# State outputs of an S5 layer in groups of 16 channels, turned back through DRAM

## The chip, the cores and the metric

The kernel runs on one core of a Trainium2 chip. The metric is the device time of one execution in microseconds. TensorE multiplies matrices (weights loaded into the array, columns streamed past them, sums in PSUM, eight banks of 512 float32 columns on 128 partitions). VectorE, ScalarE and GpSimd do the elementwise work; SyncE (SP) and ScalarE issue DMAs.

## The reference, cut to what matters

Two layers on 528 tokens (16 meta tokens and 512) of width 1024. Each layer is: half an FFN, a projection `x @ w_in` that feeds three mixers (attention with latent q and kv, a short gated convolution, an S5 state space branch), a gated merge, and half an FFN. All in float32.

```python
def s5_branch(u, a_re, a_im, log_dt, b_re, b_im, c_re, c_im, d, w_glu, b_glu, w_out):
    ...   # ab = exp(dt * a), bb = coef * b, both complex
    bu_re = jnp.einsum('gnh,blgh->blgn', bb_re, uf)
    bu_im = jnp.einsum('gnh,blgh->blgn', bb_im, uf)
    _, _, xr, xi = lax.associative_scan(_ssm_combine, elems, axis=1)
    y = (jnp.einsum('ghn,blgn->blgh', c_re, xr) - jnp.einsum('ghn,blgn->blgh', c_im, xi) + d * uf)
    y = jax.nn.gelu(y.reshape(B, L, S5_WIDTH))
    y = y * jax.nn.sigmoid(y @ w_glu + b_glu)
    return y @ w_out
```

There are 32 groups of 16 channels with 64 complex states each.

## The kernel before, in words

Features lie on partitions, tokens along the free dimension, in two halves of 264. Every large product takes its weights in chunks of 128 output features: SP loads a chunk into one of two raw buffers (L481), ScalarE rounds it (`round_ahead`, L1318), GpSimd makes the rest (`split`, L611), and TensorE makes three products (rounded by rounded, rounded by rest, rest by rounded; `product`, L696). The rounded weights sit in four slots, so ScalarE works three chunks ahead. Semaphores order everything; each engine has a program of its own, written out in the order in which it runs.

The S5 branch cuts the 528 tokens into 66 chunks of 8 steps. State inputs of a chunk are made from an input that eight small DMAs have stacked on partitions (`u8`, L1605; `s5_states_in`, L986). VectorE scans over the 66 chunks (L2245) and turns the states back, four pairs of groups at a time (`scan_turned_back`, L2248). The output of a chunk has two parts: a Toeplitz part from the eight steps of the same chunk, and a part from the state at its start. The Toeplitz kernels are made by `s5_toeplitz` (L1016), on all 128 channels of a tile at once with zeros between the groups, just before the tenth of twelve convolution chunks, and ScalarE copies them (`take_toeplitz`, L1561) into `K`, which VectorE has cleared (L2456). `s5_outputs` on TensorE (L1030) makes, for each of four tiles of 128 channels, the Toeplitz products (L1044, 128-column weights) and the state products (L1051, 32-column weights), both with the step along the free dimension. VectorE adds the skip term `d * u` (L2309), ScalarE applies Gelu in place, VectorE splits the result into rounded and rest (L2316, L2317), and TensorE goes on with `values` (V of the attention, L1076) and `glu` (L719).

The parts of the chain that the change and the prediction's steps touch:

- TensorE, in `conv` (L998): twelve chunks; `CONV_PAIR` gives each a pair of PSUM banks, and a chunk waits (`conv_taken`) until VectorE has taken the chunk that used the pair before. Chunk 12 uses the pair of chunk 10.
- VectorE, L2444 to L2467: for each tile of the convolution `conv_first` (copies the first chunk of the tile) and `conv_tile`; between them `scan_turned_back`, `latents_begin` (two reciprocals, L2293 and L2295) and, behind the last tile, `latent_tiles` (L2297).
- The tables: `tables_beside` (L2054) places the steps of the input tables (`in_step`), of the turning factors (`turn_step`) and of the output tables (`out_step`, L2176) beside the first FFN's tiles. The first FFN has three parts with 6, 8 and 8 tiles; the tables' transposes (`turn_inputs`, L950) stand behind the down products of part 2.
- SP's order of loads (L558 to L595), GpSimd's order of splits (L649 to L663), ScalarE's order (L1590 to L1652).

## Time and profile before

| | us |
|---|---|
| median of 3 runs | 2581.45 (2578.11 to 2581.68) |
| span of the profiled execution, whose own time is this span | 2579.4 |
| TensorE busy | 2543.4 |
| VectorE busy | 1414.7 |
| ScalarE busy | 953.8 |
| GpSimd busy | 1223.7 |
| first layer, end of the ninth convolution chunk to first GLU product | 54.1 |

The profile is one execution. Its timeline gives the start and length of the instructions of an engine, merged where neighbours are of the same kind; a bracket holds the idle time before them and what ended it. A float32 product appears as two instructions.

### The profile page before, as it was taken

The numbers are of one execution on the slowest core, as the hardware profiler recorded it, in microseconds if no ns is written. First come the engines' busy times: TensorE is split into PE (matmuls) and PEld (weight loads), VectorE is DVE, ScalarE is ACT, GpSimd is POOL, SyncE is SP. The second block draws the span as 40 slices with busy tenths as digits, with TensorE's granted clock in tenths as the row PEclk, the third lists the DMA queues.
The fourth block names the chain that finished last, engine by engine and source line by source line (L and its number), as shares of the span: only waits on it lengthen the run. The fifth ranks groups of instructions, "written<-read, shape, count | busy, mean of one in ns | idle before, by whom it ended". The sixth has DMA issues, their size and how long they took to land.

```text
span 2579.4 us, 51328 instructions
## 1 busy us (share of the span) xinstructions
PE 2543.4 (99%) x20356; PEld 2420.4 (94%) x20356; DVE 1414.7 (55%) x2475; ACT 953.8 (37%) x1694; POOL 1223.7 (47%) x708
## 2 busy tenths in 40 slices
PE   9999999999999999999999999999999999999997
PEld 9999999998899999999999999999977788989897
DVE  6665433874453484535576654339744535835356
ACT  4222224235532242636352222242355322437363
POOL 4444434413234456868554444354132345568582
PEclk9999999999999999999999999999999999999998
DMA  5333333312233333333233323333122333334332
GB/s 165 92 92 88 90 90 91 91 28 66 53 84 89 95 91 98 95 102 100 82 110 97 92 82 92 88 91 94 26 66 54 83 98 98 92 86 127 82 99 82
DMA packets 457391, 227.16 MB, mean 88 GB/s; under 512 B 42385, under 2 KB 456337, under 8 KB 457201
## 3 DMA queue, kind: packets, MB, share of 16 engines
q1 hardware_dynamic: 450880, 217.09, 30.9%
q10 hardware_dynamic: 6320, 7.41, 1.1%
q8 instruction: 135, 2.21, 0.4%
q14 instruction: 56, 0.45, 0.1%
HBM read 220.20 MB, written 2.10 MB: 86 GB/s over the span
## 4 chain that ended last, share of the span: by engine, by line
PE 92%; DVE 3%; issue 2%; POOL 1%; ACT 1%; DMA 0%; ACTq 0%; POOLq 0%; DVEq 0%; SPq 0%
PE ps L696 64%; PE ps L830 14%; PE ps L806 4%; PE ps L719 3%; PE ps L1044 1%; PE ps L1129 1%; PE ps L1168 1%; POOL w_lo L611 1%; PE ps L1133 1%; PE ps L1051 1%; PE ps L1144 1%; DVE ln_in L1856 0%; ACT ln_in L1300 0%; DMA w_raw<-in_ffn_w_gate 0%; PE ps L1146 0%
## 5 line engine op out<-in xcount | busy, mean ns | idle before, releaser
L611 POOL TENSOR_TENSOR w_lo<-w_raw,w_hi 128x1024 fp32r<-128x1024 f32 (+4 forms) x400 | 851.3, 2135 | 1135.9 <-ACT w_hi L1300 1135.5
L1300 ACT ACTIVATE w_hi<-w_raw 128x1024 fp32r<-128x1024 f32 (+4 forms) x400 | 372.7, 936 | 640.5 <-PE ps L696 401.6
L696 PE MATMUL ps<-x_hi,w_hi 128*128 128x264 f32 (+2 forms) x2720 | 396.5, 296 | 0.3 <-ACT w_hi L1300 0.3
L696 PE MATMUL ps<-x_hi,w_lo 128*128 128x264 f32 (+2 forms) x2720 | 389.3, 293 | 0.8 <-POOL w_lo L611 0.8
L696 PE MATMUL ps<-x_lo,w_hi 128*128 128x264 f32 (+2 forms) x2720 | 389.0, 293 | 0.0
L696 PEld LDWEIGHTS ps<-x_hi,w_hi 128*128 128x128 f32 x2720 | 355.1, 188 | 14.5 <-issue 0.8
L696 PEld LDWEIGHTS ps<-x_hi,w_lo 128*128 128x128 f32 x2720 | 355.3, 188 | 11.5 <-POOL w_lo L611 1.7
L696 PEld LDWEIGHTS ps<-x_lo,w_hi 128*128 128x128 f32 x2720 | 355.4, 188 | 9.8
L1896 DVE TENSOR_TENSOR ps<-hid_rest,ps 128x528 f32<-128x528 f32 (+1 forms) x56 | 39.7, 710 | 238.4 <-PE ps L696 226.8
L696 PE MATMUL ps<-hid_hi,w_hi 128*128 128x264 f32 (+1 forms) x1008 | 158.2, 301 | 0.1
L696 PE MATMUL ps<-hid_hi,w_lo 128*128 128x264 f32 (+1 forms) x1008 | 156.6, 299 | 0.0
L696 PE MATMUL ps<-hid_lo,w_hi 128*128 128x264 f32 (+1 forms) x1008 | 156.4, 299 | 0.0
L611 POOL TENSOR_TENSOR w_lo<-w_sum,w_hi 128x512 fp32r<-128x512 f32 x90 | 118.7, 1324 | 78.0 <-ACT w_hi L1300 77.5
L611 POOL TENSOR_TENSOR w_lo<-w_pair,w_hi 128x512 fp32r<-128x512 f32 x108 | 145.1, 1359 | 9.7 <-ACT w_hi L1300 9.7
L696 PEld LDWEIGHTS ps<-hid_hi,w_hi 128*128 128x128 f32 x1008 | 137.1, 188 | 6.7 <-DVE ln_in L1917 0.5
L696 PEld LDWEIGHTS ps<-hid_hi,w_lo 128*128 128x128 f32 x1008 | 137.2, 188 | 6.3
L696 PEld LDWEIGHTS ps<-hid_lo,w_hi 128*128 128x128 f32 x1008 | 136.9, 188 | 6.2
L1300 ACT ACTIVATE hid_rest<-ps 128x528 f32 (+2 forms) x88 | 51.0, 603 | 176.4 <-PE ps L696 163.8
L2415 DVE SCALAR_TENSOR_TENSOR stat<-stat,ps 128x528 f32<-128x528 f32 (+1 forms) x32 | 22.2, 695 | 158.1 <-PE ps L696 158.1
L1300 ACT ACTIVATE w_hi<-w_sum 128x512 fp32r<-128x512 f32 x90 | 56.4, 631 | 101.1 <-DVE w_sum L1960 66.7
L830 PE MATMUL ps<-turned_lo,w_hi 128*128 128x264 f32 (+1 forms) x576 | 92.6, 283 | 0.0
L830 PE MATMUL ps<-turned_hi,w_hi 128*128 128x264 f32 (+1 forms) x576 | 92.5, 282 | 0.0
(352 smaller groups left out, 4397.8 us busy)
## 6 DMA issues: line engine op xcount, KB each, us to landing
w_raw<-in_w_in SPq DMA_DIRECT2D x82, 512.0 KB, 3.9
w_raw<-in_ffn_w_down SPq DMA_DIRECT2D x64, 512.0 KB, 3.7
w_raw<-in_ffn_w_up SPq DMA_DIRECT2D x56, 512.0 KB, 3.8
w_raw<-in_ffn_w_gate SPq DMA_DIRECT2D x48, 512.0 KB, 3.8
w_pair<-in_ffn_w_gate SPq DMA_DIRECT2D x40, 512.0 KB, 5.2
w_pair<-in_ffn_w_up SPq DMA_DIRECT2D x32, 512.0 KB, 5.2
w_raw<-in_ffn_w_down SPq DMA_DIRECT2D x32, 384.0 KB, 3.3
w_raw<-in_w_o SPq DMA_DIRECT2D x16, 512.0 KB, 3.7
```

The lines of the kernel that those rows point to most:

```text
L611: pool.tensor_tensor(held(w_lo, c), src, held(w_hi, c).bitcast(f32), ALU.subtract).then_inc(w_split, 1)
L696: ins = nc.tensor.matmul(dst, wk, x[:, k0 + k, tokens], start=first and k == 0 and n == 0, stop=last and k == n_tiles - 1 and n == 2)
L719: ins = nc.tensor.matmul(dst, held(w, c + j, k * P, (k + 1) * P), x[:, k, tokens], start=k == 0 and n == 0, stop=k == nk - 1 and n == 2)
L806: ins = nc.tensor.matmul(ps[:, bank, 0:sp.half], held(w, c + d, k * P, (k + 1) * P), x[:, k, sp.halves[h]], start=p == 0 and k == 0, stop= ...
L830: ins = nc.tensor.matmul(ps[:, banks + bank, 0:sp.half], held(w, c + n, k * P, (k + 1) * P), x[:, k], start=start and i == 0 and k == 0, s ...
L1044: nc.tensor.matmul(ps[:, a + bank, (s0 - lo) * NC:4 * NC], K[:, m, j, :], ug[:, s0 - j:up - j, m, :], start=j == 0, stop=False, skip_group ...
L1051: ins = nc.tensor.matmul(ps[32 * q:32 * q + 32, a + s // 4, (s % 4) * NC:(s % 4 + 1) * NC], cl[:, s, ri, p * 32:(p + 1) * 32], X[:, ri, p, :],
L1129: ins = nc.tensor.matmul(ps[0:nq, j % 2, 0:q0 + nq], qT[:, b, q0:q0 + nq], kT[:, b, 0:q0 + nq], start=True, stop=True)
L1133: ins = nc.tensor.matmul(ps[0:nq, h, 0:HALF], qT[:, b, q0:q0 + nq], kT[:, b, h * HALF:(h + 1) * HALF], start=True, stop=True)
L1144: nc.tensor.transpose(ps[:, 2 + buf, k * P:(k + 1) * P], pr[:, buf, k * P:(k + 1) * P], ident[:])
L1300: return nc.scalar.activation(out, in_, f, **kw)
L1896: st.done(tt(up, gate, up, MUL))
```

## The change

The Toeplitz kernels are made earlier, for groups of 16 channels alone: on TensorE ahead of part 3 of the first FFN (`s5_kernels`), each from 64 rows of states. ScalarE copies them to `Kc` (`take_kernels`), and 16 DMAs on SP's queue, placed between the loads of convolution chunks, lay them out as the block Toeplitz matrices `T` that GpSimd has cleared. The skip term is added into the kernels by eight products with the identity. In `s5_outputs` the eight steps of a group lie stacked on the partitions, so that the Toeplitz part takes 32-column weights out of `T` with the stacked input, and the state part works on 64 rows at a time. ScalarE applies Gelu from PSUM into the stacked layout; two DMAs write it to DRAM, and eight, four on ScalarE's and four on SP's queue, read it back with channels on partitions. VectorE's output table steps have 256 elements in place of 512 and stand beside part 2's tiles; the K/V latent tiles come before the copy of chunk 10, the q latent tiles before the last tile of the convolution. The banks of V change.

```diff
-V_BANK = [6, 7, 4, 5, 0]
+V_BANK = [4, 5, 2, 3, 0]
...
+        def turn_back(eng, l, steps):
+            eng.wait_ge(y_out, (l + 1) * 2 * 16)
+            by_step = y_there.rearrange("(s h) q m c -> s q h (m c)", s=TC)
+            for s in steps:
+                eng.dma_start(ug[:, s].rearrange("p m c -> p (m c)"), by_step[s]).then_inc(y_back, 16)
...
+            def toeplitz(l, x):
+                if x == 0:
+                    sp.wait_ge(k_taken, l * 2 + 2)
+                    sp.wait_ge(t_zero, l + 1)
+                for s in range(TC):
+                    sp.dma_start(T[s::TC, x, :, s * GROUP:TC * GROUP],
+                                 Kc[32 * x:32 * x + GROUP, :, 0:(TC - s) * GROUP]).then_inc(t_in, 16)
...
                 for m in range(MT):
+                    if m in (1, 2):
+                        toeplitz(l, m - 1)
                     for n, c0 in enumerate((C_XBAR, C_C, C_B)):
...
+                    if m == 3:
+                        turn_back(sp, l, range(4, 8))
                     load(l, B_GLU + m, 0, MT * P, rows(t["s5_w_glu"], l, 0, MT, m * P, P), MT)
...
+                    if c == B_CONV + 2:
+                        pool.wait_ge(f_ready, l * MT + MT)
+                        pool.memset(T[:], 0.0).then_inc(t_zero, 1)
...
+                        if part == len(PARTS) - 1 and j == 1:
+                            pe.wait_ge(k_taken, l * 2 + 2)
...
+                        if part == len(PARTS) - 1:
+                            s5_kernels(l)
                         gate_up(l, bu, n0, t0, part, nf)
...
+            def s5_kernels(l):
+                pe.wait_ge(cl_ready, l + 1)
+                pe.wait_ge(skip_made, l + 1)
+                pe.wait_ge(lf_taken, l * 8 + 8)
+                where = [(q2, x, g) for q2 in range(2) for x in range(2) for g in range(2)]
+                for q2, x, g in where:
+                    out = ps[32 * x:32 * x + GROUP, 4 + 2 * q2 + g, :].rearrange("p (m k) -> p m k", m=MT)
+                    qg = 2 * (2 * q2 + x) + g
+                    nc.tensor.matmul(out[:, :, 0:GROUP], ident[:, GROUP * qg:GROUP * (qg + 1)], skip[:], start=True,
+                                     stop=False, skip_group_check=True)
+                for m in range(MT):
+                    for ri in range(2):
+                        for q2, x, g in where:
+                            p, r = 4 * m + 2 * q2 + x, slice(64 * g, 64 * g + 64)
+                            ins = nc.tensor.matmul(ps[32 * x:32 * x + GROUP, 4 + 2 * q2 + g, m * P:(m + 1) * P],
+                                                   bbar[r, ri, p * GROUP:(p + 1) * GROUP],
+                                                   cl[r, ri, p].rearrange("p s h -> p (s h)"),
+                                                   start=False, stop=ri == 1, skip_group_check=True)
+                ins.then_inc(k_ready, 1)
+
+            def s5_outputs(l):
+                pe.wait_ge(t_in, (l + 1) * 2 * TC * 16)
+                for m in range(MT):
+                    a = 2 + 2 * (m % 2)
+                    if m < 2:
+                        pe.wait_ge(conv_taken, l * 3 * MT + (6 + m))
+                    else:
+                        pe.wait_ge(gelu_done, l * MT + (m - 1))
+                    for g in range(2):
+                        for q in range(4):
+                            for t in range(4):
+                                nc.tensor.matmul(ps[32 * t:32 * t + 32, a + g, q * NC:(q + 1) * NC],
+                                                 T[:, q % 2, (q // 2 * 2 + g) * MT + m, 32 * t:32 * t + 32], u8[:, 2 * q + g, m],
+                                                 start=q == 0, stop=False, skip_group_check=True)
+                    pe.wait_ge(scan_back, l * MT + (m + 1))
                     for q in range(4):
                         p = 4 * m + q
                         for ri in range(2):
...
+                            for t in range(4):
+                                for g in range(2):
+                                    r = slice(64 * g, 64 * g + 64)
+                                    ins = nc.tensor.matmul(
+                                        ps[32 * t:32 * t + 32, a + g, q * NC:(q + 1) * NC],
+                                        cl[r, ri, p, 2 * t:2 * t + 2].rearrange("p s h -> p (s h)"), X[r, ri, p, :],
+                                        start=False, stop=ri == 1, skip_group_check=True)
                     ins.then_inc(y_ready, 1)
...
-                pe.wait_ge(lat_ready, l * 5 + 5)
-                pe.wait_ge(y_taken, l * MT + MT - 1)
-                pe.wait_ge(conv_taken, l * 3 * MT + 3 * MT)
+                pe.wait_ge(lat_ready, l * 5 + 2)
+                pe.wait_ge(gelu_done, l * MT + MT)
+                pe.wait_ge(conv_taken, l * 3 * MT + 3 * MT - 1)
...
-                    if n == 9:
-                        take_toeplitz(l)
...
+                    if n == 3 * MT - 1:
+                        for m in range(MT):
+                            act.wait_ge(y_ready, l * MT + (m + 1))
+                            a = 2 + 2 * (m % 2)
+                            ACTV(u8[:, :, m].rearrange("p (q g) c -> p g q c", g=2),
+                                 ps[:, a:a + 2, 0:4 * NC].rearrange("p g (q c) -> p g q c", q=4),
+                                 ACT.Gelu_apprx_tanh).then_inc(gelu_done, 1)
+                            if m % 2:
+                                act.wait_ge(gelu_done, l * MT + (m + 1))
+                                act.dma_start(y_there[:, :, m - 1:m + 1].rearrange("p q m c -> p q (m c)"),
+                                              u8[:, :, m - 1:m + 1].rearrange("p q m c -> p q (m c)")).then_inc(y_out, 16)
+                        turn_back(act, l, range(4))
...
-                nc.vector.reciprocal(stat[:, 3], stat[:, 3])
-                conv_first(l, 3)
-                st.done(nc.vector.reciprocal(stat[:, 4], stat[:, 4]))
+                nc.vector.reciprocal(stat[:, 4], stat[:, 4])
+                st.done(nc.vector.reciprocal(stat[:, 3], stat[:, 3]))
...
-                dve.memset(K[:], 0.0).then_inc(k_zero, 1)
...
                 latents_begin(l, st)
+                latent_tiles(l, 1, st)
+                conv_first(l, 3)
+                latent_tiles(l, 0, st)
                 conv_tile(l, 3, st)
-                latent_tiles(l, 0, st)
-                latent_tiles(l, 1, st)
                 s5_outputs(l, st)
```

## Rows read from the trace of the kernel before

**Rows 1.** The page, part 1: busy us (share of span) xinstructions.
```profile
PE 2543.4 (99%) x20356; PEld 2420.4 (94%) x20356; DVE 1414.7 (55%) x2475; ACT 953.8 (37%) x1694; POOL 1223.7 (47%) x708
```

**Rows 2.** Windows: us; PE, PEld, DVE, ACT, POOL busy (x); PEclk, DMA share, GB/s; both layers.
```profile
523.30:577.40 54.10, 53.82 (x847) 48.58 (x847) 37.60 (x49) 17.61 (x35) 6.64 (x5) 1.00 0.07 19
1810.90:1865.00 54.10, 53.82 (x847) 48.58 (x847) 37.62 (x49) 17.59 (x35) 6.64 (x5) 1.00 0.07 20
```

**Rows 3.** Timeline of PE, first layer: start us, us, engine, line, op, out<-in, count.
```profile
523.30 3.73 PE L1024 MATMUL ps<-s_out,s_bbar_states 128*32 128x256 f32 x64
...
544.47 4.34 PE L1044 MATMUL ps<-s_u,s_toeplitz 128*128 128x264 f32 x24
548.74 2.05 PE L1051 MATMUL ps<-s_state,s_out 128*32 128x66 f32 x128
...
569.86 0.51 PE L1076 MATMUL ps<-w_hi,ckv_hi 128*128 128x512 f32 x1
...
577.43 0.48 PE L719 MATMUL ps<-s_y_hi,w_hi 128*128 128x264 f32 x2 [0.30 <-ACT v L1300]
```

**Rows 4.** Timeline of DVE, first layer, 500 to 573 us.
```profile
502.31 3.47 DVE L2456 MEMSET s_toeplitz<- 128x4096 f32 x1 [0.92 <-DVE stat L2201]
...
524.48 0.70 DVE L2217 TENSOR_TENSOR conv_rest<-stat,ps 128x528 f32<-128x528 f32 x1
...
526.54 0.43 DVE L2253 TENSOR_TENSOR s_back<-s_state,s_turns_re 128x264 f32<-128x264 f32 x1
...
529.12 3.40 DVE L2293 RECIPROCAL stat<-stat 128x528 f32<-128x528 f32 x1
533.06 0.71 DVE L2201 TENSOR_SCALAR stat<-ps 128x528 f32<-128x528 f32 x1 [0.55 <-PE ps L696]
533.81 3.45 DVE L2295 RECIPROCAL stat<-stat 128x528 f32<-128x528 f32 x1
...
552.43 0.70 DVE L2301 TENSOR_TENSOR ckv_raw<-ckv_raw,stat 128x528 f32<-128x528 f32 x1
...
556.34 1.64 DVE L2309 SCALAR_TENSOR_TENSOR s_u<-s_u,par,ps 128x528 f32<-128x528 f32 x2
...
570.68 0.72 DVE L2316 TENSOR_SCALAR s_y_hi<-s_u 128x528 fp32r<-128x528 f32 x1
...
572.59 0.69 DVE L2316 TENSOR_SCALAR s_y_hi<-s_u 128x528 fp32r<-128x528 f32 x1
```

**Rows 5.** Timeline of PE, the products of the state inputs.
```profile
453.63 3.96 PE L986 MATMUL ps<-s_u_stacked,s_in 128*64 128x66 f32 x128
```

**Rows 6.** Timeline of ACT: issues of the stacking DMAs, and a Gelu.
```profile
434.13 5.96 ACTq L1605 DMA_DIRECT2D s_u_stacked<-s_u  x8
...
557.13 0.65 ACT L1300 ACTIVATE s_u<-s_u 128x528 f32<-128x528 f32 x1 [16.33 <-DVE s_u L2309]
```

**Rows 7.** Timeline of DVE in the first FFN: a tile of part 2, an output step.
```profile
187.97 0.71 DVE L1896 TENSOR_TENSOR ps<-hid_rest,ps 128x528 f32<-128x528 f32 x1 [4.67 <-PE ps L696]
...
236.45 4.70 DVE L2187 TENSOR_TENSOR s_tmp<-s_lambda,s_out 128x512 f32<-128x512 f32 x4
```

**Rows 8.** DMA issues: out<-in, engine, op, count, KB each, median us to landing.
```profile
w_raw<-in_w_in SPq DMA_DIRECT2D x82, 512.0 KB, 3.9
...
s_u_stacked<-s_u ACTq DMA_DIRECT2D x16, 132.0 KB, 4.1
...
out_T<-ln_in SPq DMA_DIRECT2D x16, 128.0 KB, 1.7
```

**Rows 9.** A gap on PE's timeline, and two windows (columns of rows 2).
```profile
404.25 0.36 PE L719 MATMUL ps<-x_hi,w_hi 128*128 128x264 f32 x1 [1.84 <-DVE ln_in L1801]
...
405.40:408.80 3.40, 3.40 (x18) 3.40 (x17) 3.29 (x9) 1.97 (x6) 2.39 (x1) 0.50 0.58 155
...
1297.00:1303.00 6.00, 3.96 (x28) 3.57 (x29) 4.74 (x12) 4.16 (x9) 2.40 (x1) 1.00 0.39 115
```

**Rows 10.** Timeline of POOL, between the projection and the convolution.
```profile
465.27 2.48 POOL L611 TENSOR_TENSOR w_lo<-w_raw,w_hi 128x1024 fp32r<-128x1024 f32 x1 [5.68 <-ACT w_hi L1300]
```

More of the change, by code:

```diff
@@ L271, in build @@
         decay, _ = new("s5_decay", [P, PAIRS])
-        bS, _ = new("s5_bbar_states", [P, 2, PAIRS * 2 * GROUP])
+        bbar, _ = new("s5_bbar", [P, 2, PAIRS * GROUP])
+        same_row, _ = new("s5_same_row", [P, GROUP])
+        skip, _ = new("s5_skip", [P, MT, GROUP])
         kr, _ = new("k_rope", [P, L])
@@ L1436, in ffn @@
                     bd = b0 + at_ + 2 * nf
+                    if w == 0 and part == len(PARTS) - 1:
+                        take_kernels(l)
                     with act.Fori(1 if part == 0 else 0, nf // 2) as i:
@@ L1920, in ffn @@
                             turn_step(l, d, st)
-                        if w == 0 and part == 1 and d in (1, 3, 5):
-                            out_step(l, (d + 1) // 2, st)
                 layer_norm(l, 2 * w, st, 0.5 / ALPHA, b0 + PART_AT[-1] + 2 * PARTS[-1][1])
@@ L2062, in tables_beside @@
                         in_step(l, f + 3, st)
[L2063 removed]
+                    if f == 5:
                         turn_step(l, 6, st)
[L2065 removed]
+                    if f == 6:
                         turn_step(l, 7, st)
[L2067 to L2070 removed]
+                    if f:
+                        out_step(l, f, st)
             s5_q = lambda k: s5p[:, k]
@@ L2148, in in_step @@
             def in_step(l, j, st):
-                own = [by_pair(bcomp[:, n]) for n in range(2)]
+                own = [by_pair(bbar[:, n]) for n in range(2)]
                 if j == 0:
-                    cmul(st, [bcomp[:, 0], bcomp[:, 1]], each(s5cf[:, 0], GROUP), each(s5cf[:, 1], GROUP), own[0],
+                    cmul(st, [bbar[:, 0], bbar[:, 1]], each(s5cf[:, 0], GROUP), each(s5cf[:, 1], GROUP), own[0],
                          own[1], GROUP)
```

136 lines of the change are left out of this document (48 added, 88 removed).

## The prediction

> **What bounds the kernel now.** TensorE is busy for 2543.4 of 2579.4 us [rows 1], so the profile was read for what sets TensorE's next start, not for busy shares. First the windows: the stretch that the change rebuilds, from the end of the ninth convolution chunk to the first GLU product, lasts 54.1 us in each layer, the same in both [rows 2]. Second TensorE's own timeline of that stretch [rows 3]: 3.7 us of Toeplitz kernels (L1024), three chunks up to 544.47 (17.4 us, 5.8 each), then the state outputs, 25.4 us (L1044, L1051), then V (L1076) for 7.3 us and a 0.3 us wait. Nothing but TensorE's own instructions lies on that path. Third VectorE's timeline [rows 4]: between the ninth chunk and the twelfth it is nearly full too, which decides what a reordering costs. The sum is made on the profiled execution, 2579.4 us, 2.05 us below the median 2581.45 of the runs; I add differences to the median. 0.2% of it, 5.2 us, is about what a measurement can tell from no change.
>
> **Removed from the path, per layer.** The kernels before chunk 10: 3.7 us. The outputs, 544.47 to 569.86: 25.4 us [rows 3].
>
> **State outputs, new.** Per tile m: 32 products with 32-column weights for the part inside a chunk of steps, and 64 products on 64 rows for the part from the states. Each float32 product is two instructions (64 products are x128 in L1051). L1051 issues 128 of them, of the same 66 columns and 32-column weights, in 1.98 us, 15.5 ns each [rows 3]; with 64-column weights 128 take 3.9 us, 30.4 ns [rows 5]. So the pace is 61 ns divided by the weight blocks that work side by side. The first part is then 64 x 15.5 ns = 1.0 us. The second is 128 x 15.5 = 2.0 us if two 64-row halves don't work together, 1.0 us if they do. No row shows 64-row halves. I take 1.2 us: the pace has followed the number of blocks twice. With 1.2 us a layer for the changes of shape (an estimate: the step from L1044 to L1051 costs some 0.1 to 0.2 us, and there are eight): 4 x 2.2 + 1.2 = 10.0 us; ends 9.2 and 13.2.
> [...]
>
> **Kernels, moved** ahead of part 3 of the first FFN, and no longer hidden by anything: TensorE is the bound there as well. 64 products of 128 columns on 16-column weights, by L1024's 58 ns for 256 columns in four blocks (3.73 us for 64) [rows 3]: 29 ns if rows and columns both count as blocks, 57 ns with two blocks: 3.7 or 7.3 us. The eight skip products, 0.5 us. Ahead of them TensorE must wait until ScalarE has copied the eighth turned table, whose transposes are its last instruction: 0.1 + 0.6 + 0.1 = 0.8 us (a ScalarE pass over as many columns is 0.65 [rows 6]). With 0.3 for shapes: 5.3 us; ends 5 and 9. ScalarE's two kernel copies (some 2.2 us each by its rate, ahead of its gate work) are due only two chunks, 11.6 us, later: nothing. Behind these copies ScalarE's next rounding waits, three chunks ahead of use: nothing.
>
> **VectorE in the first FFN.** Seven output steps move from the down products and part 3 into part 2's gate/up, at half the elements: about half of 6.1 us (4.70 + 1.4) a step, less than the 4.67 us that it idles a tile [rows 7]; TensorE needs its result only a tile later. The 512-wide multiplication falls away. Nothing; if a step were not covered, 1 us for each.
>
> **The order behind chunk 9 is where the change pays.** Chunk 12 uses the pair of banks that chunk 10 filled, and may start when VectorE has taken chunk 10 (`conv_first(l, 3)`). That copy now stands behind both reciprocals and the two K/V latent tiles. VectorE, freed of a 3.47 us memset, takes chunk 9 as it ends, at 523.3; 2.1 us later (524.48 to 526.54) comes the turn back, 2.6 us with the memsets (526.54 to 529.12), two reciprocals 6.85, two latent tiles 3.9 (552.43 to 556.34), the copy 0.7, a signal 0.1 [rows 4]: 539.55. TensorE, without the kernels, is through chunk 11 at 523.3 + 11.6 = 534.9. Idle 4.65 us; GpSimd's split at that time can lengthen it by some 1 us. I take chunk 12 from 540.0 to 545.8; before it ended at 544.5. So the 3.7 us are lost again and 1.3 more.
>
> **From the last output to GLU.** Outputs end at 545.8 + 10.0 = 555.8. V's banks are the outputs' own, so it waits for the fourth Gelu (0.65 and two signals, 0.9): 556.7. V takes 7.3 us. Beside it runs a chain that the old kernel didn't have, from 556.7: write of 540 KB to DRAM, 3.7 (a 512 KB load lands in 3.9, bound 3.4 to 4.5); eight reads of 132 KB, four on SP's and four on ScalarE's queue; the split of tile 0, 1.95 (570.68 to 572.59) [rows 4]. For the reads: below, four ScalarE issues at 0.745 us each (5.96 for eight) and 1.7 us for the last to land, 4.7; above, the eight same-sized copies of the stacked input, last issue 439.3 plus 4.1, 9.3 us from the first [rows 6, 8]. I take 8.5, nearest to the second row, which is the same pieces in the same number. 0.1 + 3.7 + 8.5 + 1.95 = 14.3: GLU starts at 571.0 instead of 577.4, TensorE idle for 7.0 us ahead of it. Queued behind ScalarE's wait for the write are the K copies, two roundings and the V copies, which by their lengths now end about 13 us behind the fourth Gelu (3.9 + 3.0 + 2.6 + 1.2 + 2.6) and are covered; behind SP's wait the fourth GLU weight, due later still.
>
> **Clock.** The granted clock was 0.50, its lower level (1.2 GHz), from 405.4 to 408.8 after TensorE had idled 1.84 us [rows 9]; in 3.4 us it does half the work, a loss of 1.7. It doesn't always fall: around 1298 us TensorE stood for 2.0 of 6.0 us at 1.00 [rows 9]. Gaps of 5 and 7 us are longer than both: I charge 1.7 for each, 3.4 us; ends 0 and 5.
>
> **Under cover.** The 4096-column clearing of T on GpSimd falls into its idle time of 5.68 us before 465.27 [rows 10]; beside it VectorE's copies may slow, 0.3 us (0 to 1.5). The 16 Toeplitz DMAs (1.2 MB) sit in SP's queue before convolution weights that ScalarE rounds two to three chunks ahead of use, and their result is due 60 us later: nothing, several us if the queue should hold weights past that. Loads at the layer's start: less than before.
>
> **Sum per layer.** 571.0 - 577.4 = -6.4; clock +3.4; kernels +5.3; clearing +0.3: +2.6. Two layers: +5.2, with rounding of the waits 2587 us, range of this case 2581 to 2592.
>
> **Rivals.**
> (A) Row halves don't work together: outputs +3.2, kernels +3.6 a layer, +13.6: 2600. For it: no row shows any. Against: two rows scale with the blocks.
> (B) The waits come out short: the reads land in 4.7 us (-3.8) and the clock holds (-3.4): -14.4, 2572; with one of them alone 2579. For it: the clock held in three gaps, and queues are empty then. Against: both idle stretches exceed the gaps that it held in.
> (C) The reads use half of the DMA engines. 512 KB in 3.9 and 128 KB in 1.7 us give 175 KB/us, 6.0 us for 1.06 MB; at half that rate 12, landing 13: +4.5 a layer, 2596. [...]
> (D) The new wait at chunk 12 grows, since GpSimd's clearing and splits hold VectorE up (the split of 2.48 us in rows 10 is such a piece): two pieces, 5 us, and 1.7 of low clock more a layer, 2600. My case is slower than before by over 0.2% from the point where VectorE's copy comes later than I set it, and faster where it comes 5 us sooner.
> That the change does not do what it says (the outputs stay above 20 us) would show as case A made worse; it has no chance of its own.
>
> **How the numbers follow.** Mine 0.35, A 0.18, B 0.27, C 0.12, D 0.08. The range 2572 to 2602 leaves out the edge of B and D. Faster by over 0.2% (below 2576.3): most of B, 0.22. Within: the rest of B and nearly half of mine and little of C, 0.26. Slower: 0.52.
>
> **What would show it.** In the profile after: outputs of 9 to 13 us instead of 25.4; kernels of 4 to 9 us ahead of part 3; a TensorE gap of 4 to 6 us before chunk 12 released by VectorE's copy; one of 5 to 9 us before GLU released by the split; granted clock 0.5 behind each. Without the gap before chunk 12 I am wrong by 5 us or more a layer, and the change is faster.

## The result: 29 us slower, and the profile after

The changed kernel takes 2610.44 us (median of four runs, 2609.40 to 2611.99) against 2581.05 us for the kernel before, run beside it: ratio 1.0117, 95% interval 1.0105 to 1.0129. It is slower by 29.4 us, where 5.5 were forecast (2587.0); the time lies 8 us above the upper end of the range.

The same lines as before the change, from the profiled execution of the changed kernel (span 2609.6 us). First the page, part 1 (columns of [rows 1]): TensorE is busy for 13.7 us less than before and still ends 30.2 us later, so nearly 44 us are new idle time.

```profile
PE 2529.7 (97%) x20836; PEld 2408.0 (92%) x20836; DVE 1377.3 (53%) x2456; ACT 949.1 (36%) x1666; POOL 1228.6 (47%) x710
```

Then windows of the first layer (columns of [rows 2]): from the start of chunk 10 to the GLU, the state outputs alone, and from V to the GLU.

```profile
527.16:590.42 63.26, 41.34 (x945) 36.87 (x943) 30.29 (x39) 11.85 (x20) 6.87 (x5) 0.83 0.19 56
552.79:573.05 20.26, 12.27 (x769) 10.42 (x768) 2.95 (x5) 1.83 (x3) 0.00 (x0) 0.90 0.11 31
573.78:590.42 16.64, 9.79 (x31) 7.47 (x31) 2.68 (x3) 6.23 (x12) 2.49 (x2) 0.71 0.38 118
```

The first window answers to [rows 2] and is 9.2 us longer than the 54.1 us there, although the kernels (3.7 us) have left it; TensorE works for 41.3 us of 63.3 in it. Where the other 22 us lie, its timeline tells (start, us, engine, line, op, out<-in, shapes, count, and in brackets the idle time before with what ended it):

```profile
261.25 0.63 PE L1058 MATMUL ps<-s_skip,ident 128*16 128x64 f32 x16 [0.78 <-ACT s_in L1342]
261.81 3.68 PE L1064 MATMUL ps<-s_out,s_bbar 64*16 64x128 f32 x128
265.42 2.22 PE L727 MATMUL ps<-x_hi,w_hi 128*128 128x264 f32 x16
...
545.28 3.72 PE L727 MATMUL ps<-x_hi,w_hi 128*128 128x264 f32 x16 [6.36 <-DVE stat L2251]
...
552.79 1.13 PE L1082 MATMUL ps<-s_u_stacked,s_toeplitz 128*32 128x66 f32 x64
553.85 1.50 PE L1092 MATMUL ps<-s_state,s_out 64*32 64x66 f32 x128
555.27 0.65 PE L1082 MATMUL ps<-s_u_stacked,s_toeplitz 128*32 128x66 f32 x27
557.48 0.77 PE L1082 MATMUL ps<-s_u_stacked,s_toeplitz 128*32 128x66 f32 x37 [1.56 <-issue]
558.18 1.13 PE L1092 MATMUL ps<-s_state,s_out 64*32 64x66 f32 x91
560.94 0.64 PE L1092 MATMUL ps<-s_state,s_out 64*32 64x66 f32 x37 [1.63 <-issue]
...
564.68 1.22 PE L1092 MATMUL ps<-s_state,s_out 64*32 64x66 f32 x101 [1.67 <-issue]
...
568.69 0.92 PE L1082 MATMUL ps<-s_u_stacked,s_toeplitz 128*32 128x66 f32 x37 [2.10 <-issue]
...
572.15 0.89 PE L1092 MATMUL ps<-s_state,s_out 64*32 64x66 f32 x37 [1.02 <-issue]
573.78 0.76 PE L1117 MATMUL ps<-w_hi,ckv_hi 128*128 128x512 f32 x1 [0.75 <-issue]
...
590.42 0.78 PE L750 MATMUL ps<-s_y_hi,w_hi 128*128 128x264 f32 x2 [6.84 <-DVE s_y_lo L2356]
```

There are three losses. TensorE waits 6.36 us for VectorE ahead of chunk 12. It stands five times, 7.98 us in all, in the midst of the state outputs, and no semaphore ends these gaps ("issue"). It waits 6.84 us ahead of the GLU. (The 0.75 us ahead of V is its wait for the fourth Gelu, which the prediction had.) In the second layer they are 6.36, 5.9 (four gaps) and 7.13 us.

The gaps in the outputs follow a count. Between two of them lie 37 + 91, 37 + 64 + 27, 101 + 27 and 37 + 91 matmuls: always 128, each with its weight load (a pair), wherever this falls inside a form. The 128 pairs from one such place to the next are called a block below. In the second layer the gaps are 128 pairs apart too, but the first comes only behind 260 pairs:

```profile
1865.10 1.46 PE L1092 MATMUL ps<-s_state,s_out 64*32 64x66 f32 x124 [1.63 <-issue]
```

So the block that began behind the first four of them, at 1859.68 us, was used up in 1.75 us without a gap; the section on e11_even comes back to this. Between gaps the pace is near what was taken (15.5 and 9.4 ns): 64 in 1.06 us (16.6 ns) and 128 in 1.42 us (11.1 ns) from start to start.

One view more bears on it, the DMA view of the window from 545.28 to 573.05 (a cell of the first two lines is 0.69 us):

```profile
DMA  0000000000000100000000001079910000000000
GB/s 0 24 0 0 0 0 0 0 0 0 0 0 0 24 0 0 0 0 0 24 0 0 0 0 24 0 207 302 269 24 0 0 0 0 0 24 0 0 0 0
...
q8 instruction: 6, 0.10, 1.5%
```

Besides the write (the block at 207 to 302) there are six instruction packets, the lone 24s. 24 GB/s through a cell of 0.69 us is 16 KB, and the page says the same (`q8 instruction: 139, 2.28, 0.4%`: 139 packets, 2.28 MB); over 128 pairs, 256 instructions, that is 64 bytes each. From 554 us on the packets lie in the half microseconds from 554.5, 558.5, 562.0, 566.0 and 569.5, one for each block, and each block starts 2.3 to 2.8 us behind its packet.

### The profile page after: what moved, and what is told of

It reads as the page before. It is cut to its first block, busy times and chain, and to the rows that moved or that the text cites. A ratio compares the mean times of both kernels' runs of the same rounds, so it can differ in the third digit from the quotient of the medians.

```text
span 2609.6 us, 52309 instructions
## 1 busy us (share of the span) xinstructions
PE 2529.7 (97%) x20836; PEld 2408.0 (92%) x20836; DVE 1377.3 (53%) x2456; ACT 949.1 (36%) x1666; POOL 1228.6 (47%) x710
## 3 DMA queue, kind: packets, MB, share of 16 engines
q8 instruction: 139, 2.28, 0.4%
## 4 chain that ended last, share of the span: by engine, by line
PE 88%; DVE 4%; issue 3%; ACT 1%; POOL 1%; DMA 1%; ACTq 0%; POOLq 0%; DVEq 0%; SPq 0%
PE ps L727 62%; PE ps L861 13%; PE ps L837 4%; PE ps L750 3%; PE ps L1170 1%; POOL w_lo L639 1%; PE ps L1209 1%; PE ps L1174 1%; PE ps L1092 1%; PE ps L1185 1%; PE ps L1082 0%; DMA s_y<-s_u_stacked 0%; ACT ln_in L1342 0%; DVE ln_in L1909 0%; PE ps L1187 0%
## 5 line engine op out<-in xcount | busy, mean ns | idle before, releaser
L727 PE MATMUL ps<-x_hi,w_hi 128*128 128x264 f32 (+2 forms) x2720 | 399.8, 297 | 14.3 <-DVE stat L2251 12.7
```

The source lines that it names most:

```text
L727: ins = nc.tensor.matmul(dst, wk, x[:, k0 + k, tokens], start=first and k == 0 and n == 0, stop=last and k == n_tiles - 1 and n == 2)
```

## The experiments

First theories. (1) VectorE's order alone makes the wait at chunk 12. (2) TensorE runs out of instructions: a block of 128 pairs comes every 3.5 to 4.0 us, whatever the work in it. Rival: a stall of fixed length that the small blocks bring. (3) The turn through DRAM sets the GLU's start, and its reads are slow because they use eight DMA engines of sixteen (case C). Rival: the pieces set their pace. All times below are medians beside runs of the kernel before (2579.5 to 2581.9 us); ratios are to that kernel.

**e1_order.** VectorE's order.

```diff
+                conv_first(l, 3)
                 latents_begin(l, st)
                 latent_tiles(l, 1, st)
-                conv_first(l, 3)
```

> Of the changed kernel only one thing is moved: VectorE's first operation of the fourth convolution tile now stands ahead of the two reciprocals and the kv latent tiles instead of behind them. Theory (the wait of 6.36 us and the half clock that follows it are the price of VectorE's order alone): TensorE's gap ahead of the last convolution chunk goes to under 0.5 us in both layers, the chunk takes 5.8 us instead of 7.5, nothing behind it grows, and the time falls by 2 x (6.4 + 1.7) = 16 us to about 2594 us. Rival (something else is as late, the weights of that chunk or the Toeplitz matrices): the gap falls but a new one of several us stands in its place or ahead of the state outputs, and the time falls by less than 8 us.

2593.16 us, ratio 1.0048 (1.0031 to 1.0064): 17.3 us less than the changed kernel. The timeline of TensorE, first layer:

```profile
545.01 1.13 PE L1082 MATMUL ps<-s_u_stacked,s_toeplitz 128*32 128x66 f32 x64
...
549.42 0.77 PE L1082 MATMUL ps<-s_u_stacked,s_toeplitz 128*32 128x66 f32 x37 [1.28 <-issue]
...
553.43 0.63 PE L1092 MATMUL ps<-s_state,s_out 64*32 64x66 f32 x37 [2.18 <-issue]
```

The outputs start at 545.01 instead of 552.79; the 7.8 us are the wait and the half clock (0.51 from 541.8 to 548.6 in the changed kernel). The gaps inside them stay. Theory 1 holds.

**e2_wide.** Twice the columns for each state matmul, the same number of instructions.

```diff
-    ps[32 * t:32 * t + 32, a + g, q * NC:(q + 1) * NC],
-    cl[...], X[r, ri, p, :],
+    ps[32 * t:32 * t + 32, a + g, q // 2 * 2 * NC:(q // 2 * 2 + 2) * NC],
+    cl[...], X[r, ri, p // 2 * 2:p // 2 * 2 + 2, :].rearrange("p a c -> p (a c)"),
```

> Each of the 256 state matmuls of a layer streams twice the columns (132 instead of 66, the states of its pair and of the neighbouring pair), with the same number of instructions; so the state outputs are not the reference's. Theory (TensorE runs out of instructions: a block of 128 weight loads and 128 matmuls every 3.3 us is all that it gets): the instructions grow by some 11 ns each, 128 x 4 x 11 ns = 5.7 us a layer, and the gaps of 1.0 to 2.2 us after every 128 pairs shrink by as much, so the stretch of the state outputs stays at 19 to 21 us and the kernel at 2608 to 2614 us. Rival (a stall of fixed length, from changing row and column blocks or from the wait for a bank): the gaps keep their 1.6 us, the stretch grows to about 26 us and the kernel to about 2622 us.

2613.67 us, ratio 1.0124 (1.0107 to 1.0141).

```profile
559.02 0.77 PE L1082 MATMUL ps<-s_u_stacked,s_toeplitz 128*32 128x66 f32 x37 [1.09 <-issue]
...
562.76 0.87 PE L1092 MATMUL ps<-s_state,s_out 64*32 64x132 f32 x37 [1.46 <-issue]
...
566.49 1.77 PE L1092 MATMUL ps<-s_state,s_out 64*32 64x132 f32 x101 [1.22 <-issue]
...
570.50 0.77 PE L1082 MATMUL ps<-s_u_stacked,s_toeplitz 128*32 128x66 f32 x37 [1.66 <-issue]
...
574.24 0.87 PE L1092 MATMUL ps<-s_state,s_out 64*32 64x132 f32 x37 [1.46 <-issue]
```

Blocks start 3.74, 3.73, 4.01 and 3.74 us apart; in the changed kernel it was 3.46, 3.74, 4.01 and 3.46. Wider columns cost less than expected: the work of the stretch grew by 1.7 us, not by 5.7. The gaps shrank by 1.1 us (6.9 against 8.0), so that the stretch is 20.9 instead of 20.3 us. The kernel is 3.2 us longer. That speaks for the theory, but with so little added work it alone doesn't decide.

**e7_fewer.** As e2_wide with every other state pair left out: the columns of the changed kernel, two thirds of its instructions.

```diff
-                    for q in range(4):
+                    for q in (0, 2):
                         p = 4 * m + q
```

> The state matmuls stream 132 columns each, as in e2_wide, but only every other one is left in, so half of the state channel pairs are left out: the columns streamed are those of the changed kernel, the pairs 512 a layer instead of 768. Theory (the number of instructions sets the stretch): four blocks of 128 pairs in place of six, 2 x 3.7 = 7.4 us less a layer, so the state outputs take 12.5 to 14 us instead of 20.2 and the kernel 2595 to 2598 us. Rival (the streamed columns, or the shape of the blocks, set it): the stretch stays within 2 us of 20 and the kernel within 4 us of 2610.

2596.65 us, ratio 1.0061 (1.0044 to 1.0077), 13.8 us less than the changed kernel.

```profile
557.58 0.87 PE L1092 MATMUL ps<-s_state,s_out 64*32 64x132 f32 x37 [1.18 <-issue]
...
561.59 0.87 PE L1092 MATMUL ps<-s_state,s_out 64*32 64x132 f32 x37 [1.49 <-issue]
...
565.32 0.87 PE L1092 MATMUL ps<-s_state,s_out 64*32 64x132 f32 x37 [1.22 <-issue]
```

Again 128 pairs from gap to gap, now 4.01 and 3.73 us; three gaps instead of five, and 13.7 us for the outputs (552.51 to 566.2). Columns did not count, instructions did.

**e6_kern3.** The convolution kernels' matmuls three times over, 384 pairs of one form in a row.

```diff
+                for m in 2 * list(range(MT)):
+                    ...  # the loop below, start=ri == 0, into the same banks
                 for m in range(MT):
```

> The changed kernel with the 64-row, 16-column matmuls of the convolution kernels done three times over (the first two times thrown away): 384 weight load and matmul pairs in a row instead of 128, at 28.8 ns each, so 128 pairs last 3.7 us. Theory (128 pairs every 3.5 to 4.0 us can be fetched): the pace is just the one that can be followed, so the added 256 pairs take 7.4 to 8.4 us a layer, gaps included, and the kernel gets 15 to 18 us longer (2626 to 2629 us). Rival (a fixed stall of 1.6 us after every 128 pairs of small blocks): 7.4 + 2 to 3 x 1.6 us, 10.5 to 12 us a layer, 2632 to 2635 us.

2625.50 us, ratio 1.0173 (1.0156 to 1.0190), 15.1 us more than the changed kernel.

```profile
262.14 7.18 PE L1059 MATMUL ps<-s_out,s_bbar 64*16 64x128 f32 x256 [0.78 <-ACT s_in L1350]
269.25 0.64 PE L1066 MATMUL ps<-s_skip,ident 128*16 128x64 f32 x16
269.81 3.68 PE L1072 MATMUL ps<-s_out,s_bbar 64*16 64x128 f32 x128
```

No gap at all. Blocks of 64 rows and 16 columns run at 28 ns a pair, 3.6 us for 128, and no gap follows: 7.6 us more a layer, where the rival wanted 10.5 to 12. The stall of fixed length is out.

**e4_noturn.** No DMA to DRAM and back.

```diff
-    act.dma_start(y_there[...], u8[...]).then_inc(y_out, 16)
...
-    turn_back(act, l, range(4))        # and SyncE's four
...
-    dve.wait_ge(y_back, (l + 1) * 16 * 8)
+    dve.wait_ge(gelu_done, l * MT + MT)
```

> The turn through DRAM is left out (two writes, eight reads and the wait for them); VectorE waits for the last Gelu and splits what lies in the channel layout, the unchanged inputs, so the output of this branch is wrong. Theory (the turn's chain of write, issue and reads sets the start of the GLU): the gap of 6.84 us (7.13 in the other layer) goes to 0 to 1 us, the GLU runs at full clock, and the kernel falls by 2 x (6.9 + 1.7) = 17 us to about 2593 us. Rival (VectorE's splits or the weights of the GLU are as late by themselves): a gap of over 3 us stays, and the time falls by less than 9 us.

2592.21 us, ratio 1.0042 (1.0028 to 1.0057), 18.2 us less than the changed kernel. TensorE's timeline:

```profile
583.79 0.48 PE L748 MATMUL ps<-s_y_hi,w_hi 128*128 128x264 f32 x2 [0.30 <-PE ps L1115]
```

The GLU follows V after 0.30 us, at full clock (1.00 from 583.8 to 590; two products in 0.48 us, 0.78 in the changed kernel at 0.50). The turn was the last cause of that gap, and priced right.

**e3_byq.** The reads cut so that sixteen engines take part.

```diff
-    by_step = y_there.rearrange("(s h) q m c -> s q h (m c)", s=TC)
-        eng.dma_start(ug[:, s].rearrange("p m c -> p (m c)"), by_step[s])
+    by_q = y_there.rearrange("(s h) q m c -> q h s (m c)", s=TC)
+        eng.dma_start(ug[16 * q:16 * q + 16].rearrange("p s m c -> p s (m c)"), by_q[q])
```

> The way back from DRAM is cut in another way: eight reads by group of 16 partitions (16 channels outermost, 8 steps of 1,056 bytes each) instead of eight by step (8 groups outermost, 16 channels each). Bytes, pieces and issues are the same. Theory (the engines are dealt out along the outermost dimension, so that eight of the sixteen worked at the reads): the reads move at 300 GB/s and more instead of 180 to 195, last 4.5 to 5.5 us instead of 8.5, TensorE's gap of 6.84 us ahead of the GLU falls to about 3.5, and the kernel falls by 2 x 3.3 = 6.6 us to about 2604 us. Rival (the pieces of 1,056 bytes or the writing into SBUF set the pace): the reads stay at 8 us or grow, since each now writes into 16 partitions alone, and the time stays within 2 us or rises.

2612.11 us, ratio 1.0120 (1.0103 to 1.0137): no gain. The DMA view from 578 to 592 us (a cell is 0.35 us), first of the changed kernel, then of this one:

```profile
DMA  0000000543355554555555555300003495289440
GB/s 18 6 0 0 0 0 0 69 51 100 118 193 190 193 187 151 187 175 184 184 193 190 187 196 190 133 18 0 0 0 113 135 338 164 76 245 160 40 42 1
```

```profile
DMA  0000000009699999999999999999749959494000
GB/s 20 18 17 18 6 0 0 0 9 91 172 341 187 169 124 148 145 106 160 139 115 166 121 139 181 166 178 190 126 120 228 240 125 258 88 128 43 1 0 0
```

In the changed kernel the reads hold half of the sixteen engines (share 0.5) and move mostly 151 to 193 GB/s. With the outer dimension 16 instead of 8 the share is 0.9 in most cells, yet most cells show only 106 to 190 GB/s, and the reads take 9.3 us from issue (580.18) to the first split instead of 8.6. So the half of the engines that case C priced was idle indeed, and putting it to work in this way buys nothing. Each read now fills 16 partitions instead of 128; whether this is the reason was not shown, since no run changes it alone. Sixteen engines onto 128 partitions were not tried, so what the eight engines cost by themselves stays open.

**e5_spread.** On e1_order: the tiles of the state outputs set between thirds of chunks 9 to 11.

```diff
+    behind = {8: [None, 0], 9: [1, 2], 10: [3]}.get(n, [])
     product(pair(CONV_PAIR[n]), c, 0, xh, xl, KD, True, True, split=(l, c),
+            behind=[lambda m=m: s5_outputs(l, m) for m in behind])
...                                     # and ScalarE's Gelus and writes, one by one
```

> Built on the kernel with VectorE's order mended (e1_order, 2593.2 us). The same state outputs, instruction for instruction, no longer stand in one piece behind the last convolution chunk: tile 0 stands after two thirds of chunk 9 of 12, tiles 1 and 2 after the first and the second third of chunk 10, tile 3 after the first third of chunk 11, and each is followed by 1.9 us or more of convolution matmuls of 120 ns. Theory (TensorE can get 128 pairs of weight load and matmul only every 3.5 to 4.0 us, and gets ahead during convolution matmuls): of the five gaps of 0.9 to 2.2 us at most two short ones are left, under 2.5 us in all, and since the turn through DRAM starts after the first third of chunk 11, the remaining 9.7 us of convolution and some 7 us of values cover most of its 17 us, so that the gap ahead of the GLU is under 2 us. From the start of chunk 10 to the GLU: 63.3 us in the changed kernel, some 37 here; the kernel 2555 to 2562 us, under the kernel before. Rival (the stall comes from changing to 32-column or 64-row blocks, whenever it is done): each tile still costs its 1.6 to 2.2 us of gaps, the kernel takes 2568 us or more.

2580.61 us, ratio 1.0002 (0.9993 to 1.0012): level with the kernel before, but not the 2555 to 2562 expected.

```profile
535.07 0.60 PE L1095 MATMUL ps<-s_state,s_out 64*32 64x66 f32 x36 [1.18 <-issue]
...
542.81 0.66 PE L727 MATMUL ps<-x_hi,w_lo 128*128 128x264 f32 x4 [0.69 <-issue]
...
564.21 0.77 PE L1120 MATMUL ps<-w_hi,ckv_hi 128*128 128x512 f32 x1 [6.35 <-DVE conv_u L2265]
```

In this layer two gaps are left, 1.87 us of 7.98, for the same instructions; in the second layer there are four, 5.1 us of 5.9, which theory 2 as it stood (a mean supply) doesn't explain. The gap ahead of the GLU is gone (it starts at 573.94, 0.30 us behind V). But a new wait of 6.35 us stands ahead of V, with the low clock behind it (0.50 from 562.2 to 569.0): V's fifth bank is freed by VectorE's product of chunk 11, and that stood behind the cq latent tiles. I had brought V forward, right behind chunk 12, without looking at where VectorE takes the bank.

**e8_halves.** e5_spread with the reads of tiles 0 and 1 sent out as soon as their write has landed.

```diff
     load(l, B_GLU, ...)                     # SyncE's queue, tile 0's weights
+    turn_back(sp, l, range(8), 0)           # tiles 0 and 1
...                                     # tiles 2 and 3 with a wait of their own
```

> e5_spread, and the way back from DRAM in two halves: the reads of tiles 0 and 1 go out on SyncE's queue as soon as their write has landed, long before tiles 2 and 3 are done, and VectorE splits tiles 0 and 1 without waiting for the rest. Theory (the turn is a chain of write 5.4, reads 8.5, split 2.5 us, of which half can lie earlier): the last half is 5.4 + 4.3 + 2 us behind the last Gelu and lies under 16.7 us of other matmuls, so that no gap over 0.5 us is left ahead of the GLU and the kernel is 0 to 4 us faster than e5_spread, at 2551 to 2558 us. Rival (smaller pieces of 528 bytes, and reads that meet the loads of the next weights, cost what is gained): the same time as e5_spread or more.

2579.29 us, ratio 0.9995 (0.9986 to 1.0005). The wait ahead of V still stands in front of what the halves could give; the run tells nothing of them.

**e9_tail.** On e5_spread: the cq latent tiles behind the splits, SyncE's reads one weight load earlier.

```diff
                 latent_tiles(l, 1, st)
-                latent_tiles(l, 0, st)
                 conv_tile(l, 3, st)
                 s5_outputs(l, st)
+                latent_tiles(l, 0, st)
...                                     # and SyncE's reads
```

> e5_spread (2580.6 us) showed a new gap of 6.35 us ahead of the values: their fifth bank is free only when VectorE has multiplied the product of chunk 11, and that operation stood behind the three cq latent tiles. Here the cq tiles stand behind the splits of the state outputs (ScalarE's last sigmoid, which overwrites a tile that they read, waits for them), and SyncE's four reads stand ahead of the load of the third GLU weight tile instead of behind it. Theory (the gap and the half clock after it are once more the price of VectorE's order): the values start within 0.8 us of chunk 12's end at full clock, 7.0 us for their 30 matmuls instead of 9.4; the gap of 6.35 us goes, a gap of 0 to 4 us ahead of the GLU comes in (the reads' end at about 561 + 2 us against the values' end at 565), and the time falls by 2 x (8.7 - 0 to 4) us, to 2563 to 2572 us, 0.3 to 0.7 per cent under the kernel before. Rival (the reads and splits are as late as the values were): the gap moves in whole to the GLU and the time stays within 4 us of 2580.

2565.45 us, ratio 0.9936 (0.9922 to 0.9949): 15 us faster than e5_spread and 0.64% faster than the kernel before. The window from chunk 10 to the GLU:

```profile
530.34:565.68 35.34, 33.29 (x753) 30.23 (x751) 24.40 (x30) 8.55 (x15) 6.45 (x5) 1.00 0.32 94
```

V follows chunk 12 at once and takes 7.4 us, the GLU waits 0.30 us, and the granted clock is 1.00 in the window; 35.3 us in place of 63.3 (tile 0, 2.5 us, now lies ahead of it). The move has a price behind the GLU, 1.37 us in each layer that e5_spread doesn't have: the first product on cq starts at 580.11, just after VectorE's last cq latent tile (ended 580.01), though the profile puts this gap down to "issue". What else is left are gaps inside the outputs, 1.7 us in the first layer and 4.6 us in the second, and one of them tells something new:

```profile
1816.39 0.88 PE L727 MATMUL ps<-x_lo,w_hi 128*128 128x264 f32 x5
1818.88 1.49 PE L727 MATMUL ps<-x_lo,w_hi 128*128 128x264 f32 x11 [1.60 <-issue]
1820.30 1.13 PE L1085 MATMUL ps<-s_u_stacked,s_toeplitz 128*32 128x66 f32 x64
1821.36 0.76 PE L1095 MATMUL ps<-s_state,s_out 64*32 64x66 f32 x53
1822.90 1.00 PE L1095 MATMUL ps<-s_state,s_out 64*32 64x66 f32 x75 [0.77 <-issue]
```

TensorE stands still in the midst of one ordinary convolution product on 128 x 128 weights, and the next gap comes 11 + 64 + 53 = 128 pairs later. Small blocks are not needed for it, only that 128 pairs were just used up fast.

**e10_tail_halves.** e9_tail and e8_halves together.

> e9_tail with the reads in two halves by state tiles, as in e8_halves (2579.3 us). Theory (half of the reads and two of the four splits lie earlier): where e9_tail has a gap ahead of the GLU, it is gone here, and the kernel takes 2561 to 2566 us. Rival (the chain ends in time in either): within 2 us of e9_tail.

2561.31 us (2559.31 to 2565.40), ratio 0.9925 (0.9912 to 0.9939), against e9_tail's 2562.31 to 2565.84. The theory expected a gain only where e9_tail had a gap ahead of the GLU, and it had none over 0.42 us. The medians are 4.1 us apart but the intervals overlap, so whether the halves bring anything is not settled.

**e11_even.** e10_tail_halves with one tile behind the first third of each of chunks 9 to 12.

```diff
-    behind = {8: [None, 0], 9: [1, 2], 10: [3]}.get(n, [])
+    behind = {8: [0], 9: [1], 10: [2], 11: [3]}.get(n, [])
```

> e10_tail_halves (2561.3 us) with the tiles of the state outputs set evenly, one behind the first third of each of chunks 9, 10, 11 and 12, so that 192 pairs of outputs and 48 of the convolution come every 8.3 us. In e5_spread and e9_tail the spreading left 1.9 us of gaps in the first layer but 4.6 to 5.1 in the second, one of them in the midst of convolution matmuls of 120 ns. Theory (128 pairs every 3.5 to 4.0 us, whatever their form): 240 pairs need 6.6 to 7.5 us, less than the 8.3 they have, so the gaps fall to under 1 us in each layer and the kernel to 2555 to 2560 us; the last turn half then has 3.9 + 7.4 us of other work behind it and may cost 0 to 1 us ahead of the GLU. Rival (the gaps come from the small blocks by themselves, some 1 us for each portion, or from something of the second layer alone): 3 to 5 us of gaps stay in the second layer and the time stays within 2 us of 2561, or rises.

2567.64 us (2563.08 to 2568.04), ratio 0.9946 (0.9933 to 0.9960): no gain, the median is 6.3 us above e10_tail_halves, though the ranges overlap. Gaps of 4.3 us in the first layer (three tiles of four) and 3.2 us in the second (two) are left:

```profile
536.57 0.60 PE L1098 MATMUL ps<-s_state,s_out 64*32 64x66 f32 x36 [1.41 <-issue]
...
546.82 0.42 PE L1098 MATMUL ps<-s_state,s_out 64*32 64x66 f32 x20 [1.25 <-issue]
```

and 2.5 and 1.4 us of a new wait ahead of GLU products, released by ScalarE's V copies, which stood behind its wait for the later write. So the mean supply is not the rule either: with 240 pairs in 8.3 us five tiles of eight still ran dry. What fits is that the single block counts: the next packet goes out about when a block begins (in the changed kernel the block from 557.48 and the packet from 558.5, 1.1 us behind; 1.1, 1.4 and 1.2 us for the three after it), and a block that is through before the next one is there leaves TensorE without work. Most tiles of 192 pairs in 2.5 us hold the greater part of one block.

Three blocks were used up as fast and no gap followed: 1.75 us in the changed kernel (the one from 1859.68), 2.2 us in e5_spread (from 524.6) and 1.9 us here (from 524.3). Each comes right behind long products, and the packet for its successor had gone out before TensorE took the block up, at 1859.0, 522.8 and 523.6. What holds everywhere is the time from a packet to the block behind it: all 61 gaps of over 0.7 us between blocks in the outputs of the changed kernel and of nine runs (e1 to e5, e7, e9 to e11) ended 2.2 to 3.1 us after a packet. So a block may be short where its successor's packet could go out early; what sends the packet isn't shown.

**e12_fine.** e10_tail_halves with each tile in three portions of 64 pairs, each followed by 16 convolution matmuls.

```diff
+    parts = [lambda k=k: s5_outputs(l, n - 7, k) for k in range(3)] if 7 <= n < 7 + MT else []
+    if parts:
+        parts[0]()
     product(pair(CONV_PAIR[n]), c, 0, xh, xl, KD, True, True, split=(l, c),
-            behind=[lambda m=m: s5_outputs(l, m) for m in behind])
+            behind=parts[1:])
...
```

> e10_tail_halves with each state output tile cut into three portions of 64 pairs (the Toeplitz part, states of channel pairs 0 and 1, states of 2 and 3), each followed by 16 convolution matmuls: twelve portions, ahead of and between the thirds of chunks 8 to 11 of 12. e11_even (2567.6 us) showed that it isn't the mean supply that counts: with 240 pairs in 8.3 us each portion of 192 pairs still had a gap of 1.3 to 1.7 us in six of eight cases. Theory, made sharper: the next block of 128 pairs is asked for only when the block before it begins, and is there 3.3 to 4.0 us later, so no single block may be through in less. Portions of 64 pairs (1.0 us) and 16 convolution matmuls (1.9 us) put 128 pairs into some 4.7 us: no gap over 0.3 us in either layer, 9 us less than e10's 3.1 + 5.8, so 2550 to 2555 us. Rival (each change to small blocks costs by itself, or every portion has its own gap): twelve changes instead of four, gaps of 5 us and more a layer, 2561 us or more.

(The "six of eight" there should be five of eight.) 2559.14 us (2558.15 to 2560.53), ratio 0.9919 (0.9906 to 0.9933). The two windows around the outputs, first of this kernel, then of e10_tail_halves:

```profile
480.00:578.00 98.00, 97.19 (x1427) 91.92 (x1425) 83.19 (x88) 26.72 (x36) 35.60 (x17) 1.00 0.37 88
1770.00:1868.00 98.00, 95.35 (x1388) 88.31 (x1386) 80.07 (x99) 29.87 (x46) 34.08 (x19) 1.00 0.37 91
```

```profile
480.00:578.00 98.00, 95.85 (x1430) 92.20 (x1430) 83.08 (x88) 27.21 (x36) 35.05 (x17) 1.00 0.38 93
1770.00:1868.00 98.00, 91.84 (x1378) 87.35 (x1376) 76.46 (x90) 28.74 (x40) 32.99 (x17) 0.98 0.35 87
```

No gap is left from the first portion to the last in either layer, for the same 768 pairs and three times as many changes of form; any 128 pairs in a row take 3.4 us or more from start to start here. So where every 128 pairs take longer than the 2.2 to 3.1 us from a packet to its block, as here and in e6_kern3's kernels, TensorE doesn't stand. The rival's gaps are out, but the time missed the 2550 to 2555 us expected: the profiled execution is 6.4 us shorter than e10's, the medians are 2.2 us apart, less than the 6 to 11 expected. Two things were overlooked. The 9 us of gaps that were to go hold 2.15 us ahead of the products on cq, the price of e9_tail's move; here 0.74 and 1.37 us of them are left. And changes of form are not free: from the first portion (515.75) to the plain thirds (551.86) the stretch takes 36.1 us, where the same instructions by their pace (64 in 1.06, 128 in 1.42, 16 of the convolution in 1.93) would take 33.1, some 0.12 us for each of 24 changes. This is the fastest kernel of the study, 0.8% under the kernel before and 2.0% under the changed one.

## Why the prediction was wrong, step by step

- **Kernels moved, 5.3 us a layer: right.** 0.78 of wait and 4.17 from 261.25 to 265.42, 4.95 us. Pairs of 64-row halves do work side by side (28.8 ns for 128 columns, 57 were taken if they don't), so case A is out. The seven output steps of VectorE and the clearing of T cost no gap on TensorE.
- **State outputs, 10.0 us a layer (9.2 to 13.2): the step that failed.** They take 20.3 us in the first layer and 18.7 in the second, 19 us of the 24 that the forecast lacked; 13.9 of the 19 are gaps. The pace per instruction was nearly right: 1.06 and 1.42 us a tile, where 1.0 and 1.2 were taken. The first layer's 768 pairs less their gaps take 12.3 us, 9.9 of them by this pace; the rest are changes of form and the lower clock that began at 569.1. What failed is the use of a row of 128 pairs [rows 3] as the pace of 768. The 128 of L1051 stand between runs of 24 matmuls of 0.18 us each (4.34 us for 24), so that 152 pairs took some 6.3 us there. In one piece, a block of 128 pairs comes every 3.5 to 4.0 us in the first layer, 27 to 31 ns a pair; e2 and e7 obey that number, e6 with 3.6 us a block has no gap, and e12 shows that the same instructions cost no gap when no block is used up faster.
- **"The outputs stay above 20 us" had no chance of its own.** It is what happened. The state matmuls took 11.1 ns each over 128 between gaps, all 768 in one piece 26.4 ns as a mean (20.26 us, gaps included). That the pace of a short row would not hold over the long run deserved a chance.
- **Chunk 12's wait, 5.1 us from 534.9 to 540.0: right in mechanism and releaser, short by 1.3.** It was 6.36 us. Two of VectorE's operations beside GpSimd's splits took 1.48 and 1.37 us instead of 0.66 and 0.49, the share that the prediction named as "some 1 us" and mostly left out. e1_order shows that the wait and its half clock together cost 17.3 us of the 29.4: the order could simply have been kept. Without it, the prediction said, I would be "wrong by 5 us or more a layer"; it was 8.6.
- **From the Gelu to the GLU, 14.3 us: 16.7.** The reads took the 8.5 us that were taken, from 579.1 to 587.7. The write took 5.4 instead of 3.7: a load in the other direction was no measure for a write in pieces of 528 bytes. The first split took 2.5 instead of 1.95. The idle time, 6.84 for 7.0 forecast, agrees only because V ran at half clock (0.50 up to 579.3) and took 9.8 us instead of 7.3.
- **Clock, 1.7 us for each gap: right for chunk 12 (7.5 us instead of 5.8), too little for the GLU in the first layer,** where the low clock (0.50 up to 596.4) reached 6 us into the work (3 us lost, by the share of 0.50); in the second it was 2.9 us (1.4 lost).
- **Case B** is refuted (the clock fell to 0.50 or 0.51 at all four gaps of 6.4 to 7.1 us, the reads weren't short), **C** true in that eight engines worked (share 0.5), which no row of before had shown, but the reads took 8.6 us and not the 13 that it priced, **D** true in its direction, 1.3 us instead of 5.

The sum, per layer: 10.3 or 8.7 for the outputs, 1.3 for the wait, 2.3 for the write and the split, less about 0.5 elsewhere (by difference, not traced), some 25 us over two layers on top of the forecast's 5.5, against 29.4 measured.

The prices add up: order 17.3 (e1_order), turn 18.2 (e4_noturn) and the gaps in the outputs 13.9 (8.0 and 5.9) make 49 us, and e12_fine, which removes or covers all three and leaves the new layout and its turn in place, gives 51.3. That is near, not a proof: e12_fine also pays for its changes of form, and each price was taken with the others in place.

## What to carry to other kernels

Where TensorE gets many short instructions in a row, count them: the pace of a burst of 128 is not the pace of 768, and here portions of 64 between long instructions left no gap where 768 in one piece left 8.0 and 5.9 us of them. Each change of form costs something as well (some 0.12 us here, an estimate from e12_fine's stretch), so no finer than needed. When work is moved past an engine's other duties, follow every bank and buffer that it frees to the place in the other engine's program where this is done, again after each repair. A chain through DRAM is no loss in itself; it needs as much other work behind it as it is long (here 16.7 us; in e9_tail, where it lay behind other work, the GLU waited 0.30 us).

## What the runs showed of the hardware

- The queue of the profile named "instruction" moved packets of 16 KB (139, 2.28 MB in the changed kernel), in the outputs one for each 128 weight load and matmul pairs. In the outputs in one piece the blocks started 3.5 to 4.0 us apart (4.6 once, in the second layer), while a packet itself held its engine for about 1.1 us (1.5% of 16 engines over 27.8 us, for six). A block behind a gap started 2.2 to 3.1 us after its packet (61 gaps of over 0.7 us in ten traces); what fills the time between isn't shown. Blocks of 128 pairs that lasted 3.6 us (e6_kern3) or 3.4 us and more (e12_fine) left no gap.
- 32-column blocks on 64 rows, two by four side by side, ran at 11.1 ns a matmul between gaps (128 in 1.42 us); four 32-column blocks on 128 rows at 16.6 ns (64 in 1.06 us).
- At a granted clock of 0.50 matmuls of 264 columns started 0.22 us apart (kernel before, 405.4 to 408.8), at 1.00 0.12 us apart (behind 408.9): 1.20 and 2.2 columns a ns. The first is the prediction's 1.2 GHz, as columns streamed; V's matmuls of 512 columns in the changed kernel give it too, 0.427 us apart at 0.50 and 0.233 at 1.00.
- The granted clock stayed at its lower level for 6.8 to 10.2 us at a time around the long gaps and the outputs, longer than the 3.4 us of [rows 9] (which the changed kernel has too, 0.50 from 1316.7 to 1320.1). Windows of the changed kernel (columns of [rows 2]):

```profile
541.80:548.60 6.80, 3.32 (x15) 3.35 (x16) 6.55 (x11) 0.00 (x0) 0.00 (x0) 0.51 0.14 41
569.10:579.30 10.20, 8.44 (x165) 6.65 (x154) 0.00 (x0) 0.61 (x1) 0.00 (x0) 0.50 0.20 56
586.20:596.40 10.20, 5.98 (x27) 6.01 (x28) 8.55 (x8) 4.74 (x8) 4.48 (x3) 0.50 0.29 73
```

  The second came amid the short gaps of the outputs, without any gap over 2.1 us.
- Reads of 1 MB in pieces of 1,056 bytes took 8.6 us on eight engines (share 0.5) into 128 partitions and 9.3 us on sixteen engines (share 0.9) into 16 partitions each.
